# Hybrid decoder step (HGRN2 and sparse attention): feature weights in two sets of four, key pages by halves, score copies spread

## What is computed

```
h = x @ w_in                     # 1024 -> qa fa ia ga | qb kb vb gb | qi ki wi
group A: HGRN2 recurrence, 4 heads, state 128 x 128
         f = lb + (1-lb)*sigmoid(fa);  key = (1-lb)*sigmoid(-fa)
         S_t = diag(f_t) S_(t-1) + key_t outer ia_t;  o_t = S_t^T silu(qa_t)
group B: sparse attention, 8 heads x 64
         scores = sum_h wi_h * relu(qi_h . ki)      # indexer, 16 heads
         keep the top k keys (128 of 512 prompt, 256 of 2056 decode)
         softmax attention over the kept keys, gate silu(gb)
y = LayerNorm(ALPHA * x + [A ; B] @ w_out)
```

## Time and profile before

| | before |
|---|---|
| median of 3 runs | 660.82 us (659.39 to 661.29) |
| the profiled execution, its own time | 661.23 us |
| its span, first to last instruction | 659.5 us |
| mean granted TensorE clock | 0.988 of full |
| TensorE busy | 633.0 us, 96% of the span |
| VectorE busy | 453.8 us, 69% |
| ACT busy | 312.6 us, 47% |
| moved by DMA | 115.51 MB, mean 175 GB/s |

### The profile page before, as it was taken

The page is one execution under the profiler, slowest core; times in us unless marked ns, Lnnn a source line. Parts: engine busy times, 40 slices in busy tenths (PEclk is TensorE's granted clock), DMA queues, the critical chain, the costliest instruction groups (busy, mean ns, idle before and its releaser), DMA issues.

```text
span 659.5 us, 14836 instructions
## 1 busy us (share of the span) xinstructions
PE 633.0 (96%) x5070; PEld 367.4 (56%) x5070; DVE 453.8 (69%) x1031; ACT 312.6 (47%) x1099; POOL 180.2 (27%) x312
## 2 busy tenths in 40 slices
PE   6979999999999999999999999999999999999995
PEld 5535444445453456777765556766446666854441
DVE  0303319999999889787687887777366997646434
ACT  3111572013454436667767677776665555610000
POOL 1641002502677231332323333323100003660000
PEclk8979999999999999999999999999999999999999
DMA  8930304305233205799999999998207102503411
GB/s 289 315 121 1 127 1 128 137 0 200 63 129 108 77 0 192 274 319 373 376 371 356 323 326 364 357 373 290 79 17 271 51 2 66 160 17 90 165 48 48
DMA packets 62253, 115.51 MB, mean 175 GB/s; under 512 B 8817, under 2 KB 22210, under 8 KB 62178
## 3 DMA queue, kind: packets, MB, share of 16 engines
q1 hardware_dynamic: 33906, 55.75, 25.0%
q0 software_dynamic: 12608, 40.67, 17.7%
q10 hardware_dynamic: 15664, 18.16, 8.5%
HBM read 106.53 MB, written 7.23 MB: 172 GB/s over the span
## 4 chain that ended last, share of the span: by engine, by line
PE 66%; DVE 12%; DMA 10%; issue 5%; SPq 3%; ACT 2%; POOL 2%; ACTq 0%; DVEq 0%; POOLq 0%
PE banks L622 20%; PE banks L1175 8%; DMA arena<-in_cache_k 8%; PE banks L903 8%; DVE wbuf L1759 3%; PE banks L888 2%; PE banks L821 2%; PE banks L853 2%; PE banks L709 2%; PE banks L770 2%; SPq L368 2%; PE banks L877 2%; PE banks L977 2%; PE banks L658 2%; DVE late L1735 2%
## 5 line engine op out<-in xcount | busy, mean ns | idle before, releaser
L622 PE MATMUL banks<-wbuf,xT 128*128 128x512 f32 (+1 forms) x448 | 150.0, 533 | 3.8 <-issue 3.7
L1403 ACT COPY arena<-banks 32x64 f32<-32x64 f32 x512 | 104.3, 204 | 44.0 <-PE banks L842 32.2
L369 POOL DMA_DIRECT2D arena<-in_cache_v x128 | 70.3, 549 | 156.2 <-issue 156.2
L622 PEld LDWEIGHTS banks<-wbuf,xT 128*128 128x128 f32 (+1 forms) x448 | 65.7, 175 | 79.7 <-issue 74.0
L1759 DVE STREAM_TRANSPOSE wbuf<-arena 128x1024 f32<-128x1024 f32 x64 | 75.3, 1217 | 12.4 <-DMA arena<-in_cache_k 12.2
L877 PE MATMUL banks<-xT,arena 128*128 128x288 f32 x256 | 66.4, 412 | 0.0
L903 PE MATMUL banks<-wbuf,xT 128*128 128x512 f32 (+1 forms) x192 | 65.0, 528 | 0.0
L877 PEld LDWEIGHTS banks<-xT,arena 128*128 128x128 f32 x256 | 47.3, 190 | 14.6 <-issue 2.4
L2131 POOL TENSOR_TENSOR arena<-arena,rope 128x64 f32<-128x64 f32 (+4 forms) x60 | 21.3, 384 | 103.5 <-ACT arena L1231 84.0
L903 PEld LDWEIGHTS banks<-wbuf,xT 128*128 128x128 f32 (+1 forms) x192 | 27.8, 172 | 30.0 <-issue 27.5
L1662 DVE MAX8 arena<-arena 128x8 f32<-128x1088 f32 x32 | 41.4, 1295 | 1.1
(11 more groups left out here) (286 smaller groups left out, 1011.5 us busy)
## 6 DMA issues: line engine op xcount, KB each, us to landing
arena<-in_cache_k SPq DMA_DIRECT2D x128, 256.0 KB, 4.8
arena<-in_cache_v POOLq DMA_DIRECT2D x128, 256.0 KB, 5.0
wbuf<-in_w_in ACTq DMA_DIRECT2D x4, 2048.0 KB, 9.6
wbuf<-in_w_in SPq DMA_DIRECT2D x2, 2048.0 KB, 14.0
arena<-in_w_in ACTq DMA_DIRECT2D x8, 512.0 KB, 8.8
wbuf<-in_w_in ACTq DMA_DIRECT2D x16, 256.0 KB
arena<-in_x_prompt SPq DMA_DIRECT2D x4, 512.0 KB, 4.1
wbuf<-in_w_out SPq DMA_DIRECT2D x1, 2048.0 KB, 10.7
```

Source lines behind the costliest of these rows:

```text
L369: e.dma_start(buf[n % 2][:, i, :], cache[bass.ds(pg, 1), 0].rearrange("a p h d -> p (a h d)")).then_inc(arrived[n % 2], 16)
L622: mm = pe.matmul(psum[a * NS:a * NS + ROWS[t], n % PB, 0:w // split], xT[:, c, t * P:t * P + ROWS[t]], wbuf[:, WB[g], c, a * w // split:(a ...
L1403: nc.scalar.copy(by_page[32 * b:32 * b + 32, i], turned_p[32 * i:32 * i + 32, b]).then_inc(p_ev, 1)
```

## The change

The feature weights become two sets of four features. A set is 512 columns and is loaded as 8 DMAs, one for each 128 rows of `w_in` (256 KB, rows of 2 KB). Set 0 is loaded before the loop: four pieces where features 0 and 1 were asked for, four more behind the last projection tiles, into four buffers `w_f` and four tiles of `ia`. Set 1 is loaded in the loop, one piece behind each of the iterations 13 to 20, into `w_f`, two tiles of `ga`, a new 2 KB column `wf_alone` and the end of the last feature. The key buffers get a semaphore for each half: SP asks for pages 0 and 1 of `n` after the first transpose of `n-2`, for pages 2 and 3 after the second, and VectorE waits before each transpose for its own half. ACT's four copies of bank 6 are made one after sequence 5, one after sequence 6 and two after sequence 7.

```diff
-        assert at[0] == KEEP2 + 1408 <= LOADED
+        LEVELS_AT = at[0]
+        wf_alone = carve(W2)
+        assert max(at[0], LEVELS_AT + len(LEVELS) * CH) <= LOADED
...
-        w_f = [carve(KC * P).rearrange("p (c n) -> p c n", c=KC) for _ in range(2)]
+        w_f = [carve(W2) for _ in range(4)]
+        FEATURE_SETS = ((W2, w_f + [ia[:, t] for t in range(1, NT + 1)]),
+                        (0, w_f + [ga[:, 0], ga[:, 1], wf_alone, aF[:, HA - 1, TOK - W2:]]))
...
-        k_in, v_in = sems("k_in", 2), sems("v_in", 2)
+        k_in, v_in = sems("k_in", 4), sems("v_in", 2)
...
+        FEATURES_FROM = UNITS.index(("f", FEATURES[3], 1))
...
-        def page_loads(e, cache, buf, arrived, n):
-            for i in range(4):
+        def page_loads(e, cache, buf, arrived, n, which=range(4)):
+            for i in which:
...
+        def key_pages(e, n, a):
+
+            page_loads(e, cache_k, k_buf, k_in[2 * (n % 2) + a], n, range(2 * a, 2 * a + 2))
...
-                page_loads(sp, cache_k, k_buf, k_in, 0)
-                page_loads(sp, cache_k, k_buf, k_in, 1)
+                for n in range(2):
+                    for a in range(2):
+                        key_pages(sp, n, a)
...
                 for n in range(2, NG):
-                    sp.wait_ge(kg_ok, 2 * (n - 1))
-                    page_loads(sp, cache_k, k_buf, k_in, n)
+                    for a in range(2):
+                        sp.wait_ge(kg_ok, 2 * (n - 2) + a + 1)
+                        key_pages(sp, n, a)
...
                     if chunks[0] == 0:
-                        pe.wait_ge(wf_in[m % 2], 16 * (m // 2) + 16)
+                        pe.wait_ge(wf_in[m // 4], 16 * KC)
...
-                        mm = pe.matmul(psum[:, FB, 0:HALF], w_f[m % 2][:, c, :], xT[:, c, half * HALF:(half + 1) * HALF],
+                        mm = pe.matmul(psum[:, FB, 0:HALF], of_set[c][:, m % 4 * P:(m % 4 + 1) * P], xT[:, c, half * HALF:(half + 1) * HALF],
...
                     if s == 5:
                         act.wait_ge(comb, 4)
-                        for k in range(4):
+                    if s >= 5:
+                        for k in ((0,), (1,), (2, 3))[s - 5]:
                             scores_in_order(nc.scalar.copy, 0, k).then_inc(s_ok, 1)
...
-                def load_wf(n):
-                    act.dma_start(w_f[n % 2], w_rows[:, :, FEATURES[n] * P:(FEATURES[n] + 1) * P]).then_inc(wf_in[n % 2], 16)
+                def feature_pieces(a, pieces):
+                    c0, places = FEATURE_SETS[a]
+                    for c in pieces:
+                        act.dma_start(places[c], w_rows[:, c, c0:c0 + W2]).then_inc(wf_in[a], 16)
...
                 act.wait_ge(comb, NSEQ)
-                load_wf(0)
-                load_wf(1)
+                feature_pieces(0, range(4))
                 act_evac(act, late_tiles(), turned_and_relu, lambda g, t: prompt_relu(g, t, 0))
+                feature_pieces(0, range(4, KC))
...
                     if kind == "f":
                         filled((kind, i, h))
-                        m = FEATURES.index(i)
-                        if h == 1 and m + 2 < len(FEATURES):
-                            load_wf(m + 2)
...
+                    if FEATURES_FROM <= n + 1 < FEATURES_FROM + KC:
+                        feature_pieces(1, [n + 1 - FEATURES_FROM])
...
                 def turn_keys(n):
-                    dve.wait_ge(k_in[n % 2], 64 * (n // 2) + 64)
                     if n >= 2:
                         dve.wait_ge(qk, q_no(n - 2) + 1)
                     for a in range(2):
                         w = slice(1024 * a, 1024 * a + 1024)
+                        dve.wait_ge(k_in[2 * (n % 2) + a], 32 * (n // 2) + 32)
                         nc.vector.transpose(kg[n % 2][:, w], k_buf[n % 2].rearrange("p g n -> p (g n)")[:, w]).then_inc(kg_ok, 1)
```

More of the change, by code:

```diff
@@ L364, in p_no @@
             return 65 * (n // 4) + 16 * (n % 4) + 16
-        def page_loads(e, cache, buf, arrived, n):
-            for i in range(4):
+        def page_loads(e, cache, buf, arrived, n, which=range(4)):
+            for i in which:
                 pg = e.value_load(pages[0:1, 4 * n + i:4 * n + i + 1], min_val=0, max_val=NPAGES - 1)
                 e.dma_start(buf[n % 2][:, i, :],
-                            cache[bass.ds(pg, 1), 0].rearrange("a p h d -> p (a h d)")).then_inc(arrived[n % 2], 16)
+                            cache[bass.ds(pg, 1), 0].rearrange("a p h d -> p (a h d)")).then_inc(arrived, 16)
+        def key_pages(e, n, a):
+            page_loads(e, cache_k, k_buf, k_in[2 * (n % 2) + a], n, range(2 * a, 2 * a + 2))
         def load_masks(e, a, groups):
@@ L401, in hybrid_step @@
         levels = levels_mem.bitcast(U8).rearrange("p (l n) -> p l n", l=len(LEVELS))
-        levels_f = arena[:, KEEP2 + 1408:KEEP2 + 1408 + len(LEVELS) * CH].rearrange("p (l n) -> p l n", l=len(LEVELS))
+        levels_f = arena[:, LEVELS_AT:LEVELS_AT + len(LEVELS) * CH].rearrange("p (l n) -> p l n", l=len(LEVELS))
         states = [carve(HA * P) for _ in range(2)]
@@ L872, in feature_half @@
                     n, m = FILL_NO["f", i, half], FEATURES.index(i)
+                    of_set = FEATURE_SETS[m // 4][1]
                     if chunks[0] == 0:
-                        pe.wait_ge(wf_in[m % 2], 16 * (m // 2) + 16)
+                        pe.wait_ge(wf_in[m // 4], 16 * KC)
                         pe.wait_ge(fill_ev, n)
                     for c in chunks:
-                        mm = pe.matmul(psum[:, FB, 0:HALF], w_f[m % 2][:, c, :], xT[:, c, half * HALF:(half + 1) * HALF],
+                        mm = pe.matmul(psum[:, FB, 0:HALF], of_set[c][:, m % 4 * P:(m % 4 + 1) * P], xT[:, c, half * HALF:(half + 1) * HALF],
                                        start=(c == 0), stop=(c == KC - 1), skip_group_check=True)
@@ L2196, in _ @@
                             pool.wait_ge(bias_ok, 1)
-                            page_loads(pool, cache_v, v_buf, v_in, 0)
+                            page_loads(pool, cache_v, v_buf, v_in[0], 0)
                     out_p, out_s = {3: (v_prompt, v_sample), 4: (k_prompt, k_sample)}.get(g, (None, None))
@@ L2218, in _ @@
                         pool.wait_ge(turned_new, 1)
-                    page_loads(pool, cache_v, v_buf, v_in, m)
+                    page_loads(pool, cache_v, v_buf, v_in[m % 2], m)
                 pool.wait_ge(v_free, NG)
```

## The result

The changed kernel took 654.58 us (median of 20 runs, 650.39 to 660.99) against 660.93 us of the kernel before in its 20 runs: ratio 0.9903, 95% interval 0.9881 to 0.9924. It is faster, by 6.3 us between the medians, where 3.8 us was forecast; 654.58 lies just under the range. The profiled execution is among the longer ones of its kernel (660.33 us, span 658.6), because TensorE's clock is at half in two more short stretches ahead of the loop; so the kernels are compared by stretches ahead of the loop and in it, not by their spans; where the clock falls inside such a stretch (e2, e13, e15, e16), it is said.

What follows compares the result with a forecast made beforehand. TensorE, busy for 96% of the span, was taken as the bound, so only its waits could shrink. Terms -0.8 (copies) -3.0 (key stops) -1.0 (value stop) +1.0 (set 1) = -3.8 us: 657.0 us against 660.82, range 655.0 to 660.5.

Steps and rivals of the forecast that it cites:

- the term of the score copies: In the indexer, ahead of the loop: spreading ACT's four copies gains 0.8 us, bounds 0 and 0.9.
- Excess 0.41 + 0.51: Relevance of sequence 7: starts 4.35 us after 6 against 3.94, lasts 2.50 instead of 1.99; together 0.9 us.
- Stops for key and value pages: In the loop: TensorE's waits for pages, 3.0 us for keys and 1.0 us for values, would be won.
- the sum with set 1: In the loop: 3.0 us of key stops and 1.0 us of value stop won, 1.0 us lost to set 1.
- Halves of the key buffers: In the loop: asking and waiting by halves wins 3.0 us of key stops, if landing times don't grow.
- The ring: Loop's key pages: transposes, requests and DMA take 14.0 us per two iterations; halves make it 11.5 us.
- halves do nothing: Rival in the loop: pages asked for earlier only queue longer, key stops stay; 659.0 us, chance 0.12.
- Rows of 2 KB: Loop's feature weights: wide rows cost 90 ns against 120 for the same bytes; the 1.0 us value stop goes.
- Set 1 in the quick iterations: Loads behind iterations 13 to 20: needs 372 GB/s, costs 1.0 us, bounds nothing and 3.8 us.
- The rivals at 346, 358 and 328 GB/s: Memory rate limits quick iterations: 346 gives 659.8 us (0.10), 358 gives 658.0 (0.10), 328 and below slower (0.06).
- Set 0 ahead of the loop: ACT's eight piece loads before the loop: cost nothing; 3.8 us if ACT's queue were full.
- the range's lower end: Whole kernel: 655.0 us, where all of 5.0 us and the copies are won but 1 us lost.

Runs made afterwards that it cites:

- e2: Kernel before with only the key buffers in halves (asked for and awaited): 664.51 us against 661.42, ratio 1.0045.
- e13: Kernel before, unchanged, profiled a second time: one execution of 669.95 us, loop 210.69 us.
- e15: Kernel before with only the key buffers in halves, second profile: one execution of 661.99 us, loop 209.88 us.
- e16: Kernel before with only the key buffers in halves, third profile: one execution of 664.25 us, loop 210.71 us.
- e7: Whole change, but VectorE waits for both halves of a key buffer before the first transpose; SP still asks by halves: 656.27 us, ratio 0.9894 to the kernel before.
- e8: Whole change, but SP asks for a key buffer only after both its transposes; VectorE waits by halves: 655.58 us, ratio 0.9875 to the kernel before.
- e5: Whole change, but each piece of feature weights loaded as two DMAs in rows of 512 B: 654.5 us, ratio 0.9857 to the kernel before.
- e9: Kernel before with only the key buffers in halves, and the loads of features 2 to 7 left out: 655.65 us against 661.1, ratio 0.9898.
- e6: Whole change without the loads of set 1: 655.49 us against 661.84 for the kernel before, ratio 0.9886.
- e11: Whole change with six of VectorE's top-k strikes moved into the loop: 653.33 us against 661.1 for the kernel before, ratio 0.9873.
- e1: Kernel before with only the spread of ACT's score copies: 659.66 us against 661.42, ratio 0.9968.
- e10: Whole change with POOL's first small load split in two DMAs: 655.41 us against 661.1 for the kernel before, ratio 0.9913.
- e12: Whole change plus POOL's load split, six strikes moved and one score copy behind the small relu: 656.08 us, ratio 0.9922 to the kernel before.
- e4: Whole change, unaltered, run again: 655.24 us against 661.42 for the kernel before, ratio 0.9924.

## Why the prediction was off, point by point

The direction and the places were right, the size was not, and the range (655.0 to 660.5 us) ended 0.4 us too high. The step that failed is the term of the score copies, at half of what it measured. Of the 2.5 us that the medians differ by more than forecast, 0.9 us are this term and 0.6 us the loop; 1.0 us was found in no stretch, and may be chance.

- **Score copies, forecast 0.8 us, measured 1.95 us in the indexer and 1.67 us up to the next work.** This is the term that failed most. "Excess 0.41 + 0.51" compared the distance of sequences 6 and 7 with that of 5 and 6, which holds a key transpose group and its neighbour doesn't. The undisturbed distance is 2.92 us, so the excess was 4.35 - 2.92 = 1.43 us and 0.51 us for the relevance itself, 1.94 us. The row itself said so: 1.37 us of idle time in brackets, until ACT's relu. The two copies left at the end give back 0.28 us, 0.21 of it as a stop, where 0.1 us was forecast.
- **Stops for key and value pages, forecast 4.0 us.** Right for the stops themselves: in the same profile 3.04 + 0.98 us became 0.20 us. A new one of 1.18 us came at iteration 28, so the loop won 3.15 us, where the sum with set 1 has 3.0; that this fits so well is in part luck, since two errors cancel. Over four loops of before it is 3.6 us, 0.4 of it the clock (e13).
- **Halves of the key buffers.** The ring was read rightly: both sides of the halves shorten it, and either is enough (e7, e8). Wrong was the step that put 3.0 us down to the halves and 1.0 us to the weights. Alone the halves cost 3 us by the medians (interval 1.1 to 4.9 us) and 1.5 us in the loop over three profiles (e2, e15, e16): the key pages' gain in the queues was paid by the weights on ACT's queue. The chance of 0.12 for "halves do nothing" didn't price this case: the landings of key pages did grow, by 1.4 us, but the harm was at another queue's loads.
- **Rows of 2 KB.** The price was right (about 30 and 90 ns a packet; 27 and 79 ns from the rows of e5 and e8), the benefit wasn't: the same 2 MB in narrow rows gives the same loop (e5). What helped was that the six loads of half a MB left the loop (e9 is as quick without them); whether by their bytes, by their size or by the time at which they were asked for, no run tells apart. The Trainium skill (DMA: Bandwidth & Descriptors, Specifications), which puts line rate at 512 B, was nearer in its consequence, though the rows show a difference of 1.3 times.
- **Set 1 in the quick iterations, forecast 1.0 us lost.** Measured: none (e6). The 372 GB/s was had: 370 GB/s from 345 to 401 us. The rivals at 346, 358 and 328 GB/s fall with it, and the about 358 GB/s for one core, which the Trainium skill (same page and section) gets by halving a stack's 716 GB/s between two cores, are exceeded over 56 us by one core alone. Nor were 374 GB/s near the most that goes: a load of 2 MB in the kernel before, alone on the engines, ran at 402 GB/s from 193 to 197 us.
- **Set 0 ahead of the loop, forecast nothing.** Right: ACT's first four requests took 2.27 us where two had taken 7.42, and the other four fitted beside its 3.61 us of idle time. (The first four pieces are 512 packets in place of 2048, a quarter and not half.)
- **Readings and sums.** Not five but seven of the loop's logits had idle time: 0.55 and 0.92 us at the first and third iteration, behind VectorE's strikes, which the change leaves alone (e11). And the range's lower end is the case in which nothing is lost: with 1 us lost the prediction's own terms give 656.0, not 655.0.
- **Not forecast.** The pause of POOL, which turned into a stop of 0.3 to 1.6 us at iteration 28 in all profiles since but e1, e10 and those of before, and the clock: a stop of 2 to 3 us in the loop can be followed by half speed.

## What to carry to other kernels

When a queue's requests are made sooner, look at the other queues that share the transfer engines: here the stop went to weights on another queue, and the part that looked best alone made the kernel slower until the weights were taken out of its way. To size what a stall costs, compare with an instance that has the same neighbours, not with the one beside it. A stop of 2 us or more in the loop cost more than its length here, since the clock fell with it, so short stops spread out were cheaper than one long. And one profile is too few to sum stops that come and go.

## What the runs showed of the hardware

- In the loop TensorE's clock was at 2.4 GHz through all stops under 1.6 us, and fell to 1.2 GHz for 3.4 or 6.8 us in or shortly after stops of 2.2 to 2.9 us (e2, e13, e15, e16). Ahead of the loop it isn't so: in the profile of after it also fell from 96 us on, just behind a stop of 0.21 us, and after 200 us, where the stops were 0.17 to 0.23 us.
- 0.001 of the mean granted clock goes with 0.6 to 0.7 us of this kernel's time, and kernels with nearly the same stretches differ in it (0.984 in e12, 0.991 in e4).
- POOL pauses 3.3 to 4.2 us between its first and second request of iteration 28 in all 18 profiles (the expectation of e10 has 2.7 to 3.4); one DMA more ahead of it doesn't move it. What it is stays open.
- With the key pages asked for by halves, at the same total rate (375 and 373 GB/s), ACT's weight loads took a median of 11.0 us in place of 6.9, the key pages 6.9 in place of 5.5 (e2, 300 to 350 us).
- Three queues together carried 370 GB/s over 56 us and 374 GB/s over 47 us.
